# All four probability heads of a sparse-attention unit scaled on VectorE, none on GpSimd

## The reference, cut to what matters

```
logits = jnp.einsum('bqhd,bqkd->bqhk', qa_b, k_sel, ...) * A_HEAD_DIM ** -0.5
logits = jnp.where(valid[:, :, None, :], logits, -jnp.inf)
p = jax.nn.softmax(logits, axis=-1)
return jnp.einsum('bqhk,bqkd->bqhd', p.astype(v_sel.dtype), v_sel)
```

## Time and profile before

| | |
|---|---|
| median of 3 runs | 3271.12 us (3264.89 to 3271.68) |
| the profiled execution, own time | 3259.0 us |
| its span | 3257.2 us |
| mean granted TensorE clock | 0.976 of full |
| sparse attention, layer 0 | about 427 to 577 us of the span |
| sparse attention, layer 1 | about 2025 to 2175 us of the span |

### The profile page before, as it was taken

The page is one execution under the profiler, slowest core; times in us unless marked ns, Lnnn a source line. Parts: engine busy times, 40 slices in busy tenths (PEclk is TensorE's granted clock), DMA queues, the critical chain, the costliest instruction groups (busy, mean ns, idle before and its releaser), DMA issues.

```text
span 3257.2 us, 39961 instructions
## 1 busy us (share of the span) xinstructions
PE 3037.6 (93%) x15032; PEld 2511.5 (77%) x15032; DVE 2091.7 (64%) x3355; ACT 1502.6 (46%) x2530; POOL 841.4 (26%) x450
## 2 busy tenths in 40 slices
PE   7998878999999999999999977889999899999998
PEld 5786765788887888878877966558887788887887
DVE  6678886342459998952448788852433799998234
ACT  5368877332344333321324788763333533334112
POOL 1121055351022222232221300634311222222221
PEclk9998999999999999999999989999999999999999
DMA  5555600431012232252254483023211122233322
GB/s 199 138 145 124 142 7 1 129 96 41 20 49 69 78 97 78 78 168 73 95 138 131 112 169 91 1 72 97 72 33 46 37 87 78 78 97 123 105 73 76
DMA packets 295983, 288.42 MB, mean 89 GB/s; under 512 B 19168, under 2 KB 258272, under 8 KB 295536
## 3 DMA queue, kind: packets, MB, share of 16 engines
q1 hardware_dynamic: 291392, 272.24, 29.3%
q10 hardware_dynamic: 4400, 13.63, 1.2%
HBM read 214.46 MB, written 71.37 MB: 88 GB/s over the span
## 4 chain that ended last, share of the span: by engine, by line
PE 73%; DVE 10%; ACT 10%; issue 3%; DMA 2%; POOL 1%; ACTq 0%; DVEq 0%; POOLq 0%
PE ps L2123 38%; PE ps L2402 8%; PE ps L2403 8%; PE ps L2404 8%; ACT above L1032 4%; PE ps L2305 2%; PE ps L2249 1%; POOL w_lo L874 1%; DVE xs_lo L1441 1%; ACT p_a L1174 1%; PE ps L2194 1%; PE ps L2376 1%; DVE p_a L1797 1%; DMA h_t<-h_spill 1%; PE ps L2195 1%
## 5 line engine op out<-in xcount | busy, mean ns | idle before, releaser
L874 POOL TENSOR_TENSOR w_lo<-raw,w_hi 128x512 fp32r<-128x512 f32 (+4 forms) x228 | 440.5, 1942 | 1167.3 <-ACT w_hi L954 1165.7
L2123 PE MATMUL ps<-xs_hi,w_hi 128*128 128x512 f32 (+1 forms) x1728 | 539.2, 393 | 25.7 <-POOL w_lo L874 14.6
L2123 PE MATMUL ps<-xs_lo,w_hi 128*128 128x512 f32 (+1 forms) x1728 | 535.0, 391 | 0.0
L2123 PE MATMUL ps<-xs_hi,w_lo 128*128 128x512 f32 (+1 forms) x1728 | 533.9, 390 | 0.0
L1829 DVE TENSOR_TENSOR h_t<-h_t,ps 128x1024 f32<-128x1024 f32 x96 | 117.2, 1221 | 524.0 <-PE ps L2123 509.7
L2123 PEld LDWEIGHTS ps<-xs_hi,w_hi 128*128 128x128 f32 (+1 forms) x1728 | 321.0, 188 | 104.3 <-issue 24.7
L954 ACT ACTIVATE w_hi<-raw 128x512 fp32r<-128x512 f32 (+4 forms) x212 | 161.6, 783 | 487.0 <-PE ps L2123 436.0
L2123 PEld LDWEIGHTS ps<-xs_lo,w_hi 128*128 128x128 f32 (+1 forms) x1728 | 324.2, 188 | 70.8
L2123 PEld LDWEIGHTS ps<-xs_hi,w_lo 128*128 128x128 f32 (+1 forms) x1728 | 324.0, 187 | 70.5
L1317 ACT ACTIVATE w_hi<-w_sum 128x512 fp32r<-128x512 f32 x210 | 133.1, 634 | 325.4 <-DVE w_sum L1968 242.0
L912 POOL TENSOR_SCALAR p_a<-p_a,rca 128x1024 f32<-128x1024 f32 (+7 forms) x96 | 179.6, 1880 | 390.5 <-DVE rca L1770 389.8
(11 more groups left out here) (345 smaller groups left out, 6411.8 us busy)
## 6 DMA issues: line engine op xcount, KB each, us to landing
raw<-in_w_gu SPq DMA_DIRECT2D x48, 512.0 KB, 4.2
act_spill<-cv SPq DMA_DIRECT2D x44, 512.0 KB, 5.9
raw<-in_w_in SPq DMA_DIRECT2D x32, 512.0 KB, 5.7
raw<-in_w_kv SPq DMA_DIRECT2D x32, 512.0 KB, 3.8
qk_spill<-t_hi SPq DMA_DIRECT2D x24, 512.0 KB, 2.7
qk_spill<-t_lo SPq DMA_DIRECT2D x24, 512.0 KB, 2.9
k_b<-qk_spill SPq DMA_DIRECT2D x32, 384.0 KB
gate_e<-in_w_gu SPq DMA_DIRECT2D x20, 512.0 KB, 4.0
```

Source lines behind the costliest of these rows:

```text
L874: nc.gpsimd.tensor_tensor(w_lo[s][:, w], raw[s][:, w], w_hi[s][:, w].bitcast(f32), ALU.subtract).then_inc(lo_done, 1)
L2123: ins = M(dst[0:c, a:b], w[s][:, k * c:(k + 1) * c], xt[:, a:b], start=(at == 0 and w is w_hi and part == 0), stop=(at == kc - 1 and w is ...
```

## The change

One constant becomes 0. All loops and waits that depend on it follow: the four scalings of a unit are all issued by VectorE, each behind the `nba` of the next head; GpSimd's loop is empty; TensorE's first TA of a unit waits for `pa_dve` alone, whose count per unit goes from one to four; and VectorE no longer waits for `pa_pool`.

```
-N_POOL = 3
+N_POOL = 0
```

## The result

The changed kernel takes 3277.22 us (median of 16 runs, 3271.29 to 3284.04), the kernel before, measured with it, 3266.26 us (16 runs, 3259.72 to 3273.56). The ratio is 1.0029, with a 95% interval of 1.0022 to 1.0037: slower, by 9.5 us (7.2 to 12.1). The profiled execution took 3271.57 us against 3259.0, its span 3269.8 against 3257.2.

The account below looks back on a forecast made before the run. VectorE was taken to bound the start of sparse attention, with gaps later; terms of 6.07 us a layer, 12.1 in all, added to the median 3271.12 gave 3283 us, range 3272 to 3296.

Parts of the forecast that it names:

- VectorE is the bound in units 0 and 1, and five scalings of 0.66 are paid in full: Units 0 and 1: VectorE's queue has no gap, so five scalings before unit 1's last bias add 3.30 us a layer.
- unit 2 would come at about 30.1 us: Sign: from unit 0's first maximum to unit 2's, the time grows from 26.8 us to about 30.1.
- Waiting for GpSimd gives nothing back: First transpose of a layer: removing TensorE's 4.3 us wait for GpSimd returns nothing, as VectorE's last scaling ends later, at 441.7.
- GpSimd's silence is worth at most 1 us: VectorE's speed without GpSimd working: gain taken as zero, with 1 us for both layers as the bound.
- the 0.4 us a layer that I named as possible: 384-wide step at 523.46, 0.83 us while GpSimd was scaling: up to 0.4 us given back once a layer.
- Gaps and hand-overs, unit 2 on: Units 2 to 10: added scalings exceed VectorE's idle gaps by 0.20 to 0.52 us a term; units 11 to 15 cost nothing.
- the gaps of 0.40 in unit 10: Unit 10: gaps of 0.40 cover scalings of 0.33; only the third is late for VA, +0.23 us.
- The clock: TensorE's clock, an unknown: VA of qb = 4 lost 1.4 us; more waiting may bring this to other blocks or move it.
- the few hundredths that I had allowed: Sign of being wrong: TensorE's granted clock in the stretch moves by more than a few hundredths.
- my fourth rival: First transpose: TensorE's 4.3 us wait for GpSimd starts the chain; up to 8.6 us return, 3262.5; chance 0.06.

Follow-up runs that it names:

- e1: Against the kernel before, VectorE scales all four heads in units 0 and 1 only, GpSimd as before from unit 2 on: 3274.48 us, ratio 1.0027.
- e3: Kernel before with GpSimd's scalings left out and nothing in their place, heads 0 to 2 unscaled: 3267.17 us, ratio 1.0007.
- e5: Changed kernel plus GpSimd multiplying a constant tile into unused memory, released by the same reciprocals: 3291.18 us, ratio 1.0078.
- e11: Changed kernel plus GpSimd multiplying a constant tile into unused memory, released by the end of VectorE's scaling: 3282.62 us, ratio 1.0043.
- e8: The changed kernel run once more, nothing altered: 3279.50 us, ratio 1.0041.
- e6: Changed kernel with unit 1's four scale_head multiplications given from VectorE to GpSimd: 3275.35 us, ratio 1.0033.
- e2: Against the kernel before, VectorE scales all four heads from unit 2 on; GpSimd keeps heads 0 to 2 in units 0 and 1: 3270.75 us, ratio 1.0009.
- e9: Changed kernel with 20 matmuls of 512 columns added on TensorE in its wait ahead of a layer's first transposes: 3280.69 us, ratio 1.0038.

## Why the prediction was right, and where it was off

I forecast +12.1 us and 3283; the change is +9.5 (7.2 to 12.1) by the ratio and +11.0 between the medians, 3277 in a series in which the kernel before was 4.9 us faster than in the runs I was shown. So 4.9 of the 6 us between 3283 and 3277 are the number I started from.

- *VectorE is the bound in units 0 and 1, and five scalings of 0.66 are paid in full.* Right, to 0.02 us (3.32 for 3.30, between the first maximum and the last bias), and e1 places it: with those 12 scalings alone unit 2 comes as late as in the changed kernel. I had written that unit 2 would come at about 30.1 us; it came at 31.4, which is these 3.3 us and the clock.
- *Waiting for GpSimd gives nothing back.* Right: in e3 unit 2 of layer 0 comes at 26.87 us as before.
- *GpSimd's silence is worth at most 1 us.* Right, and my reading of the earlier trace rows was: the 384-wide step went from 0.83 and 0.82 us to 0.41, so the 0.4 us a layer that I named as possible were held up by GpSimd. But I took an undisturbed full stretch for more than it was. e5 and e11 show that it is a matter of when GpSimd's instruction starts against VectorE's step. In the kernel before the mask step stood 0.07 us ahead of GpSimd's instruction at 430.11:

```profile
430.04 0.68 DVE L1719 TENSOR_SCALAR tie_next<-score,thr_i 128x896 f32<-128x896 f32 x1
```

That this order is what protected the kernel before is argued, not tested: e5 and e11 use another GpSimd instruction.

- *Gaps and hand-overs, unit 2 on.* Right in sum, less so one by one. VectorE's first maxima are a poor mark within a pair of units, since some of them lie off the path (unit 5's comes another 0.7 us late, and unit 6's has 0.2 of it back); the start of the VA, for which TensorE needs all copies of a block, is a better one. Against e1, which scales from unit 2 on as the kernel before does and has the same clock up to the VA of qb = 2, the changed kernel is later by:

| stretch | summed | measured, layer 0 / layer 1 |
|---|---|---|
| unit 2 to VA of qb = 7 | 0.30 | 0.29 / 0.28 |
| to VA of qb = 6 (units 3, 4) | 0.43 | 0.19 / 0.17 |
| to VA of qb = 5 (units 5, 6) | 0.92 | 0.90 / 0.89 |
| to VA of qb = 4 (units 7, 8) | 0.49 | 0.28 / 0.29 |
| to VA of qb = 3 (units 9, 10) | 0.63 | 0.96 / 0.88 |
| to VA of qb = 2 (units 11, 12) | 0 | -0.01 / 0.00 |

The rows behind one line of it, e1 first and then the changed kernel (19.48 and 20.38 us from VA to VA):

```profile
494.72 6.23 PE L2307 MATMUL ps<-pt_a,va 128*64 128x512 f32 x28
...
514.20 5.37 PE L2307 MATMUL ps<-pt_a,va 128*64 128x512 f32 x24
```

```profile
492.11 6.23 PE L2305 MATMUL ps<-pt_a,va 128*64 128x512 f32 x28
...
512.49 5.37 PE L2305 MATMUL ps<-pt_a,va 128*64 128x512 f32 x24 [0.43 <-issue]
```

The line for units 7 and 8 is where the 0.42 us of the mask step came back. Units 9 and 10 cost 0.3 us more than summed: the gaps of 0.40 in unit 10 covered less of the scalings of 0.33 than I had counted on. Why is not shown.

- *The clock.* I named it as an unknown and gave it no term in the sum. Over the whole stretch the granted clock hardly moved (0.92 and 0.94 before, 0.91 and 0.92 after), within the few hundredths that I had allowed; in the first two units it fell from 0.87 and 0.94 to 0.78 in both layers. In the profiles it took 1.2 and 1.3 us at unit 1's end (layers 0 and 1). It gave 1.6 us a layer back around the VA of qb = 4, whose 20 matmuls took 4.51 us and not 5.86 and 6.15. And in layer 0 it gave 1.0 back in units 2 and 3: 1.5 in the transposes of unit 2, of which the kernel before had made up 0.5 by unit 4. Without it the layers would stand at 6.1 and 6.0 us, against 6.07 summed. With it they stand at 4.7 and 5.6, so the clock takes 1.8 us off the 12.1. That it was so little is luck: single episodes are worth 1.0 to 1.7 us, of either sign, and e8 shows one more of 1.7 us in another execution of the same kernel.

The Trainium skill's rule on the shared ports (page "SBUF — State Buffer", section "SBUF: two separate sides") stood beside my fourth rival. This change showed a gain of 0.4 us a layer in one step, and none in the first two units. Of the two halves of the rule, e5 and e11 agree with the one: who starts first keeps the port, and the other waits. With the other half, that the port is held for the whole instruction, e5 does not agree: a step that came half a microsecond into GpSimd's 3.3 us was held up by 0.86, not by the 2.8 that were left. In e6, where GpSimd reads two inputs, a step was held up by 1.69 us of an instruction of about 2.2, which is nearer to it.

Open: what in the course of a unit lets TensorE's clock fall at unit 1's end in one kernel and not in another. Filling one wait did not settle it.

## What to carry to other kernels

Count a moved instruction by where it lands in the receiving engine's queue: the 12 scalings of units 0 and 1 put 3.3 us a layer on the path and the other 84 only 2.7 to 2.8, because the queue had no gap in the first place and gaps in the second. The medians of e1 and e2 (+8.8 and +2.9 us) make the difference look larger, since TensorE's clock is in both. An idle engine is no gain by itself, and giving it work can slow its neighbour; in e5 that cost about 12 us, and in e11, where the end of VectorE's scaling released it, 2 to 4. When a few us are to be explained, line up one event per unit across the kernels; it separates queue time from clock time where a median of runs cannot.

## What the runs showed of the hardware

- A GpSimd multiplication of 128x1024 from SBUF to SBUF (3.3 us) held up VectorE's next step by 0.78 to 0.86 us when that step began 0.5 to 0.7 us after it, and was itself stretched to 4.76 us when VectorE's scan had begun 0.18 us ahead (e5, e11). Four GpSimd multiplications with two inputs of 128x1024 took 8.74 us, and under them a 0.62 us step was held up for 1.7 (e6). A 384-wide step took 0.83 us beside GpSimd's scalings and 0.41 without them.
- The same 25 matmuls kept TensorE busy for 5.37 us at a granted clock of 0.50 and for 2.94 us at 1.00. In e9 twenty matmuls of 512 columns right ahead of the first transposes had these at full clock (8 in 1.03 us, before 1.94), and not the 16 transposes 8 us later (3.24 and 3.62 us).
- The same 12 matmuls took 2.80 us in one execution and 4.49 in another of the same kernel (granted clock 1.00 and 0.62; the changed kernel and e8).
